# A three-block transformer kernel: the mask of the sparse attention by threshold, rank and scan, and the weight splits before it on another engine

## The chip, the cores and the metric

The kernel runs on one core of one Trainium2 chip. The metric is the device time of one execution in microseconds (us); it was measured three times. An "engine" below is one of the core's five: PE (TensorE, matmuls), DVE (VectorE), ACT (ScalarE), POOL (GpSimd) and SP (SyncE, here only the queue that issues the weight loads).

## The reference

The program computes, for 512 tokens of width 1024, a stack of blocks in float32: an even mixer, a feed-forward layer, an odd mixer, another feed-forward layer, and then two layers of a second block. Only the odd mixer is touched. Cut to what matters:

```python
cq, ckv, kr, ik, iw = _split(h @ w_in, (512, 256, 64, 64, 8))
cq, ckv = _rms_norm(cq, q_norm), _rms_norm(ckv, kv_norm)
qf = (cq @ w_qb).reshape(B, T, 8, 128 + 64)          # per head: nope part, rope part
qi = (cq @ w_iq).reshape(B, T, 8, 64)                # index queries, rope on the first 32
ki = _layer_norm(ik, ik_g, ik_b)                     # index keys, rope on the first 32
def block(c):                                        # 128 queries at a time
    isc = einsum('bqh,bqhs->bqs', wi, relu(einsum('bqhd,bsd->bqhs', qi, ki)))
    isc = where(kpos <= tq, isc, -1e30)
    _, idx = lax.top_k(isc, 128)                     # of equal scores the earliest keys win
    g = kv_cat[idx]
    pr = masked_softmax(einsum('bqhc,bqkc->bqhk', qa, g), idx <= tq)
    return einsum('bqhk,bqkc->bqhc', pr, g[..., :256])
```

Every query may look at its 128 best keys by the index score. The kernel does not gather keys: it computes attention over all earlier keys and adds a mask (0 for a chosen key, -1e30 for another).

## The kernel before

**Weights.** Every product is done as three matmuls on a high and a low part of each operand (lines 595 to 597, `mm3`). SP loads a weight tile into `wraw`, ACT copies its high part to `whi` (line 1318, `split`), and another engine subtracts it to give the low part `wlo`: POOL at line 3128 or DVE at line 2074. Which of the two it is stands in the plan of the weights (`weight_plan`, lines 309 to 399): an item has `low="pool"`, `"dve"` or `"both"`. PE waits for the low part before it uses the tile. Two tiles of 2048 columns fit, so tile n+2 is split once PE has used tile n. Each engine's program walks the same list of items (`Slots`), and `prepare` issues the splits whose buffers are free at that point of that engine's own instruction order; nothing else orders them.

**The odd mixer.** Five programs (`odd` in the tensor, scalar, vector, gpsimd and sync programs) are written out by hand and meet at semaphores. In order:

- `o_in`: the first projection; DVE and POOL then make the index keys (`kk`, slot 1) and the rope part of the keys (slot 0).
- `o_tm`, the index-query half ("iq"): four products of 128 tokens each. ACT copies each out of its bank ("iq raw"), DVE applies the rotation (`rope`, lines 2339 to 2352: six TENSOR_TENSOR and a COPY), PE transposes the result (`turn_index_query`, line 1074) and ACT copies it to `qi`. The raw buffers and the rotated buffers are two deep, so token tile 2 needs the transpose of tile 0.
- `o_tm`, the "q" half: four products more. Transposes of the index queries stand between them. POOL rotates these queries (`rotate`, lines 3157 to 3169, six TENSOR_TENSOR each).
- the transposes of `kk` (line 1067), ACT's copy of the index keys (`kiT`), and index scores for query block 1 (128 queries against 256 keys): per head a small matmul (line 1136), a Relu on ACT into `rl`, a multiply-add on DVE (lines 2873, 2876) into the score rows. Blocks 2 (384 keys) and 3 (512 keys) follow; query block 0 needs no choice.
- `work`: the products with `o_q_nope` (`o_qn`), `o_w_uk` and `o_w_uv`, woven between the index scores.
- `best_keys(q, c)`: 16 rounds of MAX (line 2887, the eight largest of each row) and MATCH_REPLACE (line 2889, overwrites those eight by -3e38 in a copy). After 16 rounds 128 keys are overwritten, and one TENSOR_SCALAR (line 2893) makes the mask from them. Block 1 is done beside the index scores of 2 and 3, block 2 directly after, block 3 one round per head inside the attention loop.
- the attention loop over 32 heads (8 per query block): PE scores (1160, 1161) and mask (1162), DVE row maximum (2922), ACT exponential (1950), PE transpose (1170), a copy by ACT or DVE, PE value product (1182).

## Time and profile before

| what | value |
|---|---|
| median of three runs | 3355.51 us (3355.22 to 3355.51) |
| the profiled execution: its own time, its span in the trace | 3355.51 us, 3353.9 us |
| PE busy, matmuls | 3236.1 us, 96% |
| DVE busy | 2029.2 us, 61% |
| ACT busy | 1457.0 us, 43% |
| POOL busy | 906.4 us, 27% |
| share of the chain that ended last | PE 78%, DVE 16%, ACT 3%, issue 1% |
| the odd mixer's stretch from the iq products to its output projection | about 829 to 1004 us |

Busy time is the time in which an instruction of the engine is recorded, waiting for a port inside an instruction included. The chain goes back from the last instruction to whatever released it. It is a mean over stages: in the feed-forward layers PE is never idle for long, while the odd mixer has waits in both directions, and only that stretch of 175 us is touched here.

### The profile page before, as it was taken

How to read it: one execution, taken by the hardware profiler on the slowest of the kernel's cores; microseconds unless marked ns; L12 is line 12 of the kernel's file. 1: busy time of each engine (PE TensorE's matmuls, PEld its weight loads, DVE VectorE, ACT ScalarE, POOL GpSimd, SP SyncE). 2: the span in 40 equal slices, each digit the busy share in tenths (PEclk: the TensorE clock that was granted, in tenths of full speed). 3: DMA queues.
4: the chain of work that ended last, by engine and by line, in shares of the span. 5: the costliest groups of instructions: out<-in, count | busy, mean ns of one | idle time of the engine just before them, and what ended most of it. 6: DMA issues, size and time to landing. Idle time of an engine off the chain costs nothing.

```text
span 3353.9 us, 47772 instructions
## 1 busy us (share of the span) xinstructions
PE 3236.1 (96%) x20092; PEld 2874.7 (86%) x20092; DVE 2029.2 (61%) x2997; ACT 1457.0 (43%) x2244; POOL 906.4 (27%) x413
## 2 busy tenths in 40 slices
PE   8999999999989999999999999999999999999998
PEld 6887899978668899888999778899899998788998
DVE  6568755445856544575747636574775576366656
ACT  4465445433534444354434324453454343235433
POOL 3210133321400333203232431323232323313232
PEclk9999999999999999999999999999999999999999
DMA  4310333331102333313222322332332323223332
GB/s 131 112 43 26 107 97 117 103 100 58 63 26 88 101 113 101 124 56 123 89 88 95 113 84 77 117 101 82 114 101 86 105 85 122 76 89 107 94 96 76
DMA packets 239815, 308.97 MB, mean 92 GB/s; under 512 B 8337, under 2 KB 168097, under 8 KB 239089
## 3 DMA queue, kind: packets, MB, share of 16 engines
q1 hardware_dynamic: 236016, 291.41, 27.1%
q0 software_dynamic: 3584, 14.52, 1.2%
q8 instruction: 158, 2.59, 0.3%
q14 instruction: 57, 0.46, 0.0%
HBM read 303.80 MB, written 2.10 MB: 91 GB/s over the span
## 4 chain that ended last, share of the span: by engine, by line
PE 78%; DVE 16%; ACT 3%; issue 1%; DMA 0%; POOL 0%; DVEq 0%; ACTq 0%
PE bank L595 24%; PE bank L597 24%; PE bank L596 24%; DVE wlo L2074 3%; ACT whi L1318 1%; DVE wraw L2096 1%; DVE raw_w L2096 1%; PE bank L974 1%; DVE xl L2147 1%; PE bank L615 1%; PE bank L1257 1%; PE bank L1248 1%; DVE ul_w L2274 1%; PE bank L1182 0%; DVE st L2105 0%
## 5 line engine op out<-in xcount | busy, mean ns | idle before, releaser
L3128 POOL TENSOR_TENSOR wlo<-wraw,whi 128x1024 fp32r<-128x1024 f32 (+3 forms) x217 | 555.0, 2561 | 1508.0 <-ACT whi L1318 1507.6
L595 PE MATMUL bank<-xh,whi 128*128 128x256 f32 (+1 forms) x2456 | 724.6, 295 | 48.6 <-DVE zt L2269 20.0
L1318 ACT ACTIVATE whi<-wraw 128x1024 fp32r<-128x1024 f32 (+3 forms) x426 | 440.6, 1038 | 675.8 <-PE bank L597 545.2
L597 PE MATMUL bank<-xh,wlo 128*128 128x256 f32 (+1 forms) x2456 | 718.7, 293 | 0.0
L596 PE MATMUL bank<-xl,whi 128*128 128x256 f32 (+1 forms) x2456 | 715.3, 291 | 0.0
L595 PEld LDWEIGHTS bank<-xh,whi 128*128 128x128 f32 x2456 | 467.3, 190 | 69.9 <-issue 28.8
L3128 POOL TENSOR_TENSOR wlo<-raw_w,whi 128x1024 fp32r<-128x1024 f32 (+1 forms) x130 | 311.6, 2401 | 723.5 <-ACT whi L1318 723.5
L596 PEld LDWEIGHTS bank<-xl,whi 128*128 128x128 f32 x2456 | 468.0, 191 | 10.3
L597 PEld LDWEIGHTS bank<-xh,wlo 128*128 128x128 f32 x2456 | 466.5, 190 | 10.5
L595 PE MATMUL bank<-whi,uh_w 128*128 128x512 f32 x1216 | 473.9, 390 | 0.0
L597 PE MATMUL bank<-whi,ul_w 128*128 128x512 f32 x1216 | 473.4, 389 | 0.0
L596 PE MATMUL bank<-wlo,uh_w 128*128 128x512 f32 x1216 | 473.1, 389 | 0.0
L1318 ACT ACTIVATE whi<-raw_w 128x1024 fp32r<-128x1024 f32 (+1 forms) x315 | 307.8, 979 | 361.6 <-PE bank L597 265.1
L2074 DVE TENSOR_TENSOR wlo<-wraw,whi 128x1024 fp32r<-128x1024 f32 (+2 forms) x209 | 243.8, 1169 | 296.0 <-ACT whi L1318 295.2
L595 PE MATMUL bank<-ah_w,whi 128*128 128x256 f32 x1296 | 367.4, 284 | 10.7 <-DVE wraw L2096 6.8
L595 PE MATMUL bank<-whi,xh 128*128 128x512 f32 (+2 forms) x976 | 371.6, 381 | 4.0 <-DVE xl L2320 2.2
L596 PE MATMUL bank<-al_w,whi 128*128 128x256 f32 x1296 | 366.6, 283 | 0.0
L597 PE MATMUL bank<-ah_w,wlo 128*128 128x256 f32 x1296 | 366.5, 283 | 0.0
L596 PE MATMUL bank<-wlo,xh 128*128 128x512 f32 (+2 forms) x976 | 366.5, 375 | 0.0
L597 PE MATMUL bank<-whi,xl 128*128 128x512 f32 (+2 forms) x976 | 366.4, 375 | 0.0
L2074 DVE TENSOR_TENSOR wlo<-raw_w,whi 128x1024 fp32r<-128x1024 f32 (+1 forms) x185 | 211.8, 1147 | 253.8 <-ACT whi L1318 253.0
L597 PEld LDWEIGHTS bank<-whi,ul_w 128*128 128x128 f32 x1216 | 228.2, 188 | 47.9
(392 smaller groups left out, 5049.0 us busy)
## 6 DMA issues: line engine op xcount, KB each, us to landing
wraw<-in_w_in SPq DMA_DIRECT2D x26, 1024.0 KB, 5.2
wraw<-in_ffn_w_down SPq DMA_DIRECT2D x20, 1024.0 KB, 5.1
raw_w<-in_ffn_w_down SPq DMA_DIRECT2D x20, 1024.0 KB, 5.1
raw_w<-in_mlp_w SPq DMA_DIRECT2D x19, 1024.0 KB, 5.1
wraw<-in_mlp_w SPq DMA_DIRECT2D x17, 1024.0 KB, 5.2
wraw<-in_ffn_w_gate SPq DMA_DIRECT2D x32, 512.0 KB, 4.8
raw_w<-in_ffn_w_gate SPq DMA_DIRECT2D x32, 512.0 KB, 5.0
raw_w<-in_ffn_w_up SPq DMA_DIRECT2D x32, 512.0 KB, 4.5
```

Source lines behind the costliest of these rows:

```text
L595: M.matmul(o, lh, rh, start=start, stop=False, skip_group_check=more)
L596: M.matmul(o, lh, rl, start=False, stop=False, skip_group_check=more)
L597: return M.matmul(o, ll, rh, start=False, stop=stop, skip_group_check=more)
L615: i = M.transpose(bank[:, j * 128:(j + 1) * 128], src[:, (f + j) * 128:(f + j + 1) * 128], ident)
L974: ins = M.matmul(o[:, 0:256], lhs, rhs, start=(br == 0), stop=(br == 2 and kk + 128 >= nk))
L1248: M.matmul(bank[:, 0:n], s.qk[:, 4 + hh, t * 128:(t + 1) * 128], s.qk[:, hh, t * 128:T], start=True, stop=True).then_inc(*made.inc(("made" ...
L1257: i = M.matmul(bank[:, q * 128:(q + 1) * 128], s.PT[:, hh % 2, o:o + 128], s.vt[:, t, hh * 128:(hh + 1) * 128], start=(t == 0), stop=(t == q))
L1318: A.activation(hi, raw, ACT.Copy).then_inc(*k.w_hi.inc(("hi", j)))
L2074: V.tensor_tensor(lo, raw, hi.bitcast(F), ALU.subtract).then_inc(*k.w_lov.inc(("lo", j)))
L2096: V.tensor_tensor(b, x, y, ALU.subtract).then_inc(*done.inc(("sum of", j)))
L2147: V.tensor_tensor(lo, ring.of((*key, f))[:, :].rearrange("p (f t) -> p f t", f=4), hi.bitcast(F), ALU.subtract).then_inc(*done.inc((*name, ...
L3128: G.tensor_tensor(lo[:, 0:n], raw[:, 0:n], hi[:, 0:n].bitcast(F), ALU.subtract).then_inc(*k.w_lo.inc(("lo", j)))
```

## The change

Four things change, all in the odd mixer.

1. The mask. The sixteenth MATCH_REPLACE and the one TENSOR_SCALAR go. In their place nine DVE instructions per query block take the 128th largest score as a threshold, mark the keys above it and count them, mark those equal to it, number the equal ones by a running sum, keep as many as are still wanted, add the two marks, turn them into 0 and -1e30, apply the causal mask to the last 128 keys and convert to bfloat16. They write the two rows of `rl`.
2. The low parts of the second `o_tm` tile and of the first `o_qn` tile, done by DVE before, are done by POOL.
3. PE transposes index-query tile n after product n+2 instead of after product n+3; ACT's copies follow.
4. ACT takes the square roots for `ckv` after the second "q" product instead of after the fourth, and POOL asks for its next weight tile before it rotates query tile 1, not after. On DVE the statistics of `ckv` stand behind the (empty) walk through the "q" products.

```diff
@@ -271,3 +271,3 @@
 
-    def slot(self, tag, view, fine=0, share=False, low="pool"):
+    def slot(self, tag, view, fine=0, share=False):
 
@@ -283,3 +283,3 @@
         else:
-            self.loads[load].items = [self.item(tag, load, 2, 0, nk, "both" if share else low)]
+            self.loads[load].items = [self.item(tag, load, 2, 0, nk, "both" if share else "pool")]
 
@@ -378,5 +378,4 @@
     add_tm("o_tm", kview("o_q_tm"), 512, 1024, fine=0)
-    plan.slot("o_tm", kview("o_q_tm")[:, :, 0:512], low="dve")
-    plan.slot("o_qn", kview("o_q_nope")[:, :, 0:512], low="dve")
-    plan.slot("o_qn", kview("o_q_nope")[:, :, 512:1024])
+    add_tm("o_tm", kview("o_q_tm"), 0, 512, fine=0)
+    add_fm("o_qn", kview("o_q_nope"), 0, 1024, 512)
     add_fm("o_uk", kview("o_w_uk"), 0, 1024, 1024)
@@ -1122,7 +1121,7 @@
         for tt, _ in enumerate(tm_units("o_tm", ("iq",), 512, x, 4)):
-            if tt > 2:
-                turn_index_query(tt - 3)
+            if tt > 1:
+                turn_index_query(tt - 2)
         for tt, _ in enumerate(tm_units("o_tm", ("q",), 512, x, 4)):
-            if tt < 3:
-                turn_index_query(tt + 1)
+            if tt < 2:
+                turn_index_query(tt + 2)
         turn_keys("ki", 1)
@@ -1863,5 +1862,4 @@
         def index_query(key, tt):
-            if tt > 2:
-                turn_index_query(tt - 3)
             if tt > 1:
+                turn_index_query(tt - 2)
                 act.wait_ge(at("iq", tt - 2))
@@ -1910,5 +1908,5 @@
         for tt, _ in enumerate(tm_units("o_tm", ("q",), query)):
-            if tt < 3:
-                turn_index_query(tt + 1)
-            if tt == 3:
+            if tt < 2:
+                turn_index_query(tt + 2)
+            if tt == 1:
                 act.wait_ge(at("o var", 1, 3))
@@ -2857,2 +2855,3 @@
         run(tm_units("o_tm", ("iq",), index_query))
+        run(tm_units("o_tm", ("q",), lambda key, tt: None))
         for tt in range(NT):
@@ -2861,3 +2860,2 @@
             root(tt, 1)
-        run(tm_units("o_tm", ("q",), lambda key, tt: None))
         for tt in range(NT):
@@ -2883,3 +2881,3 @@
             n = (q + 1) * 128
-            full, left, top = isc[q], wkk[:, c, 0:n], o.m8[:, c, :]
+            full, left, top, cn = isc[q], wkk[:, c, 0:n], o.m8[:, c, :], o.cn
             for r in range(16):
@@ -2888,7 +2886,24 @@
                 dve.wait_ge(done.now())
-                V.match_replace(left, top, left if r else full, -3.0e38).then_inc(*done.inc(("left over", q, r)))
                 if r < 15:
+                    V.match_replace(left, top, left if r else full, -3.0e38).then_inc(*done.inc(("left over", q, r)))
                     yield
-            dve.wait_ge(at("left over", q, 15))
-            V.tensor_scalar(o.mb[q], left, -2.0e38, -1e30, ALU.is_gt, ALU.mult).then_inc(*done.inc(("mb", q)))
+            thr = top[:, 7:8]
+            gt, eq = rl[:, 0, 0:n], rl[:, 1, 0:n]
+            V.tensor_scalar(gt, full, thr, 0.0, ALU.is_gt, ALU.add, accum_out=cn[:, 0:1]).then_inc(*done.inc())
+            dve.wait_ge(done.now())
+            V.tensor_scalar(cn[:, 1:2], cn[:, 0:1], -1.0, 128.0, ALU.mult, ALU.add).then_inc(*done.inc())
+            V.tensor_scalar(eq, full, thr, None, ALU.is_equal).then_inc(*done.inc())
+            dve.wait_ge(done.now())
+            V.tensor_tensor_scan(left, o.one[:, :].to_broadcast([128, n]), eq, 0.0, ALU.mult, ALU.add).then_inc(*done.inc())
+            dve.wait_ge(done.now())
+            V.scalar_tensor_tensor(left, left, cn[:, 1:2], eq, ALU.is_le, ALU.mult).then_inc(*done.inc())
+            dve.wait_ge(done.now())
+            V.tensor_tensor(gt, gt, left, ALU.add).then_inc(*done.inc())
+            dve.wait_ge(done.now())
+            V.tensor_scalar(gt, gt, -1.0, 1e30, ALU.add, ALU.mult).then_inc(*done.inc())
+            d = gt[:, n - 128:n]
+            dve.wait_ge(done.now())
+            V.tensor_tensor(d, d, con[:, C_CM:C_CM + 128], ALU.min).then_inc(*done.inc())
+            dve.wait_ge(done.now())
+            V.tensor_copy(o.mb[q], gt).then_inc(*done.inc(("mb", q)))
             yield
@@ -3257,4 +3272,4 @@
         slots.done()
-        rotate(1)
         slots.get("o_qn")
+        rotate(1)
         rotate(2)
```

The order of instructions shows what the plan makes of this. "waits" names the semaphores: `s_w_hi` is ACT's high part, `s_w_lo` the low part from POOL, `s_w_lo_half` the one from DVE. On POOL, behind the rotation of the keys (COPY wkk_o), before:

```order
L3242 COPY wkk_o<-wkk_o 128x4x64 [waits s_pool_out]
L3160 TENSOR_TENSOR gb<-zv_o,cs 128x256 [waits s_act_out]
L3161 TENSOR_TENSOR gb<-zv_o,cs 128x256
L3163 TENSOR_TENSOR X_o<-gb 128x8x32 [waits s_pool_out]
L3165 TENSOR_TENSOR gb<-zv_o,cs 128x256 [waits s_pool_out]
L3166 TENSOR_TENSOR gb<-zv_o,cs 128x256
L3168 TENSOR_TENSOR X_o<-gb 128x8x32 [waits s_pool_out]
L3160 TENSOR_TENSOR gb<-zv_o,cs 128x256 [waits s_dve_out,s_act_out,s_pool_out]
```

And after:

```order
L3257 COPY wkk_o<-wkk_o 128x4x64 [waits s_pool_out]
L3143 TENSOR_TENSOR wlo<-wraw,whi 128x2048 [waits s_w_hi] x2
L3175 TENSOR_TENSOR gb<-zv_o,cs 128x256 [waits s_act_out]
L3176 TENSOR_TENSOR gb<-zv_o,cs 128x256
L3178 TENSOR_TENSOR X_o<-gb 128x8x32 [waits s_pool_out]
L3180 TENSOR_TENSOR gb<-zv_o,cs 128x256 [waits s_pool_out]
L3181 TENSOR_TENSOR gb<-zv_o,cs 128x256
L3183 TENSOR_TENSOR X_o<-gb 128x8x32 [waits s_pool_out]
L3143 TENSOR_TENSOR wlo<-wraw,whi 128x2048 [waits s_w_hi,s_pool_out]
L3175 TENSOR_TENSOR gb<-zv_o,cs 128x256 [waits s_dve_out,s_act_out]
```

Two splits of 2048 columns now stand in front of the rotation of query tile 0 (the first TENSOR_TENSOR on `zv_o`), and the split of the second `o_qn` tile, which stood behind the rotation of tile 1, stands in front of it.

On DVE, from the last copy of the index keys through the rotation of index-query tile 0 (`X_o`), before:

```order
L2822 COPY wkk_o<-wkk_o 128x4x64 [waits s_dve_out]
L2074 TENSOR_TENSOR wlo<-wraw,whi 128x2048 [waits s_w_hi]
L2343 TENSOR_TENSOR rsc_o<-X_o,cs 128x128 [waits s_act_out]
L2344 TENSOR_TENSOR rsc_o<-X_o,cs 128x128
L2346 TENSOR_TENSOR X_o<-rsc_o 128x8x16 [waits s_dve_out]
L2348 TENSOR_TENSOR rsc_o<-X_o,cs 128x128 [waits s_dve_out]
L2349 TENSOR_TENSOR rsc_o<-X_o,cs 128x128
L2351 TENSOR_TENSOR X_o<-rsc_o 128x8x16 [waits s_dve_out]
L2832 COPY X_o<-X_o 128x8x32 [waits s_dve_out]
L2343 TENSOR_TENSOR rsc_o<-X_o,cs 128x128 [waits s_act_out]
```

And after:

```order
L2820 COPY wkk_o<-wkk_o 128x4x64 [waits s_dve_out]
L2341 TENSOR_TENSOR rsc_o<-X_o,cs 128x128 [waits s_act_out]
L2342 TENSOR_TENSOR rsc_o<-X_o,cs 128x128
L2344 TENSOR_TENSOR X_o<-rsc_o 128x8x16 [waits s_dve_out]
L2346 TENSOR_TENSOR rsc_o<-X_o,cs 128x128 [waits s_dve_out]
L2347 TENSOR_TENSOR rsc_o<-X_o,cs 128x128
L2349 TENSOR_TENSOR X_o<-rsc_o 128x8x16 [waits s_dve_out]
L2830 COPY X_o<-X_o 128x8x32 [waits s_dve_out]
L2341 TENSOR_TENSOR rsc_o<-X_o,cs 128x128 [waits s_act_out]
```

The split in front of the rotation is gone (so is a second one in front of tile 3).

On DVE at the end of the choice for query block 1, where `rl_o` holds the marks, `gb` the scores, the threshold and the counts, and `wkk_o` the running sum; before:

```order
L2887 MAX gb<-wkk_o 128x8 [waits s_dve_out]
L2889 MATCH_REPLACE wkk_o<-gb,wkk_o 128x256 [waits s_dve_out]
L2893 TENSOR_SCALAR mb_o<-wkk_o 128x256 [waits s_dve_out]
L2887 MAX gb<-gb 128x8
L2889 MATCH_REPLACE wkk_o<-gb 128x384 [waits s_dve_out]
```

And after (the running sum is printed as a SCALAR_TENSOR_TENSOR on one_o):

```order
L2885 MAX gb<-wkk_o 128x8 [waits s_dve_out]
L2892 TENSOR_SCALAR rl_o,gb<-gb 128x256 [waits s_dve_out]
L2894 TENSOR_SCALAR gb<-gb 128x1 [waits s_dve_out]
L2895 TENSOR_SCALAR rl_o<-gb 128x256
L2897 SCALAR_TENSOR_TENSOR wkk_o<-one_o,rl_o 128x256 [waits s_dve_out]
L2899 SCALAR_TENSOR_TENSOR wkk_o<-wkk_o,gb,rl_o 128x256 [waits s_dve_out]
L2901 TENSOR_TENSOR rl_o<-rl_o,wkk_o 128x256 [waits s_dve_out]
L2903 TENSOR_SCALAR rl_o<-rl_o 128x256 [waits s_dve_out]
L2906 TENSOR_TENSOR rl_o<-rl_o,con 128x128 [waits s_dve_out]
L2908 CAST mb_o<-rl_o 128x256 [waits s_dve_out]
L2885 MAX gb<-gb 128x8
L2888 MATCH_REPLACE wkk_o<-gb 128x384 [waits s_dve_out]
```

Two instructions give way to nine, and all but the third wait for the one before them. Behind them stands the first MAX of block 2 as before; the same happens with 384 and 512 columns.

## Rows read from the trace of the kernel before

**Rows 1.** Waits of PE, 820 to 1010 us: total, times, longest (us).
```profile
PE bank L1182 <- DVE X_o L2325: 6.1, 5, 2.4
PE bank L1136 <- ACT kiT_o L1507: 2.3, 1, 2.3
...
PE bank L1136 <- DVE xl L2320: 1.9, 1, 1.9
```

**Rows 2.** Timeline of PE, 829 to 860 us: start, duration, line, instruction [idle before].
```profile
829.15 0.50 PE L595 MATMUL bank<-whi,xh 128*128 128x512 f32 x1 [2.23 <-DVE xl L2320]
...
840.46 0.60 PE L1074 MATMUL bank<-con,X_o 128*128 128x128 f32 x4
...
853.72 1.04 PE L1067 MATMUL bank<-con,wkk_o 128*128 128x128 f32 x8
857.09 2.00 PE L1136 MATMUL bank<-kiT_o,qo_o 64*128 64x256 f32 x16 [2.34 <-ACT kiT_o L1507]
```

**Rows 3.** Timeline of DVE, 832 to 870 us.
```profile
832.20 0.42 DVE L2814 TENSOR_TENSOR zv_o<-zv_o,par 128x256 f32<-128x256 f32 x1
...
834.90 2.28 DVE L2074 TENSOR_TENSOR wlo<-wraw,whi 128x2048 fp32r<-128x2048 f32 x1
...
838.80 0.30 DVE L2832 COPY X_o<-X_o 128x256 f32<-128x256 f32 x1
...
845.28 0.82 DVE L2343 TENSOR_TENSOR rsc_o<-X_o,cs 128x128 f32<-128x128 f32 x1
...
850.08 0.29 DVE L2832 COPY X_o<-X_o 128x256 f32<-128x256 f32 x1
...
856.78 3.94 DVE L2787 TENSOR_SCALAR zv_o<-zv_o,rs 128x256 f32<-128x256 f32 x1
...
862.02 0.34 DVE L2873 TENSOR_SCALAR gb<-rl_o,wi_o 128x256 f32<-128x256 f32 x1
862.47 4.02 DVE L2876 SCALAR_TENSOR_TENSOR gb<-rl_o,wi_o,gb 128x256 f32<-128x256 f32 x7
```

**Rows 4.** Timeline of POOL, 840 to 905 us.
```profile
844.57 1.39 POOL L3160 TENSOR_TENSOR gb<-zv_o,cs 128x256 f32<-128x256 f32 x1 [12.67 <-ACT zv_o L1507]
...
856.02 4.55 POOL L3128 TENSOR_TENSOR wlo<-wraw,whi 128x2048 fp32r<-128x2048 f32 x1 [0.91 <-ACT whi L1318]
...
887.90 4.64 POOL L3128 TENSOR_TENSOR wlo<-wraw,whi 128x2048 fp32r<-128x2048 f32 x1 [13.61 <-ACT whi L1318]
892.49 1.19 POOL L3160 TENSOR_TENSOR gb<-zv_o,cs 128x256 f32<-128x256 f32 x1
...
900.20 2.41 POOL L3128 TENSOR_TENSOR wlo<-wraw,whi 128x1024 fp32r<-128x1024 f32 x1 [1.44 <-ACT whi L1318]
```

**Rows 5.** Timeline of DVE, 888 to 895 us.
```profile
889.25 4.97 DVE L2876 SCALAR_TENSOR_TENSOR gb<-rl_o,wi_o,gb 128x512 f32<-128x512 f32 x2 [1.56 <-ACT rl_o L1507]
```

**Rows 6.** The last MATCH_REPLACE line: ns min/median/max, first and last start, forms.
```profile
L2889 DVE MATCH_REPLACE8 wkk_o<-gb,wkk_o x45: 407/543/678, 868.4 to 953.0; 128x256 f32<-128x256 f32 x15, 128x384 f32<-128x384 f32 x15, 128x512 f32<-128x512 f32 x15
```

**Rows 7.** Timeline of ACT, 829 to 860 us: the high parts of the two tiles.
```profile
830.67 1.90 ACT L1318 ACTIVATE whi<-wraw 128x2048 fp32r<-128x2048 f32 x1
...
840.71 1.92 ACT L1318 ACTIVATE whi<-wraw 128x2048 fp32r<-128x2048 f32 x1 [0.98 <-PE bank L597]
```

**Rows 8.** The line that made the mask.
```profile
L2893 DVE TENSOR_SCALAR mb_o<-wkk_o x3: 293/360/426, 900.0 to 953.7; 128x256 bf16<-128x256 f32 x1, 128x384 bf16<-128x384 f32 x1, 128x512 bf16<-128x512 f32 x1
```

**Rows 9.** The running sum of the even mixer, the one scan of this form.
```profile
L2427 DVE TENSOR_TENSOR_SCAN og_e<-gb,og_e x1: 1212/1212/1212, 68.7 to 68.7; 4x512 f32<-4x512 f32 x1
```

**Rows 10.** Timeline of DVE, 920 to 960 us, the attention loop.
```profile
923.35 0.29 DVE L2922 TENSOR_REDUCE nm_o<-bank 128x1 f32<-128x128 f32 x1 [2.81 <-PE bank L1162]
...
937.41 0.42 DVE L2922 TENSOR_REDUCE nm_o<-bank 128x1 f32<-128x256 f32 x1 [0.78 <-PE bank L1162]
...
956.36 0.56 DVE L2922 TENSOR_REDUCE nm_o<-bank 128x1 f32<-128x384 f32 x1 [1.56 <-PE bank L1162]
```

**Rows 11.** Stretch: length, busy PE, PEld, DVE, ACT, POOL; granted clock, DMA share, GB/s.
```profile
860.00:880.00 20.00, 17.97 (x63) 11.24 (x64) 18.68 (x51) 8.07 (x18) 4.94 (x7) 0.83 0.09 26
```

More of the change, by code:

```diff
@@ L3257, in odd @@
         slots.done()
+        slots.get("o_qn")
         rotate(1)
-        slots.get("o_qn")
         rotate(2)
```

## Prediction

> **What bounds the kernel now.** The profile's page says PE 96% busy and PE 78% of the last chain, so outside the odd mixer DVE or POOL time costs nothing. I therefore went on with the waits of PE in the mixer's stretch, 820 to 1010 us: it waits for DVE's copy in the attention loop (6.1 us in five waits), for the index keys (2.3 us) and for a DVE result before the index scores of block 2 (1.9 us) [rows 1]. So here the chain jumps between PE and DVE. Next the timelines. From 829.15 the four iq products take 11.31 us, 2.83 each, with no gap; the transposes of the keys start at 853.72 [rows 2]. Up to there PE is dense: whatever holds PE before 853.72 is paid in full. The DVE rows show which operation is late: TENSOR_TENSORs of the rotation of tile 3 take 0.82 us each, and a TENSOR_SCALAR of 256 columns 3.94 us where the same form beside it takes 0.34 [rows 3].
>
> **The mechanism that carries the forecast.** Set these beside POOL. The 3.94 us end at 860.72; POOL's split of 2048 columns runs from 856.02 to 860.57 [rows 3, 4]. At 889.25 two SCALAR_TENSOR_TENSORs take 4.97 us together, and POOL's next split runs from 887.90 to 892.54 [rows 4, 5]. So a DVE instruction of such a form, issued while POOL is inside one instruction, stands until that one ends, whatever its length; when both have a queue they alternate (rotation of tile 3: 845.28 to 850.37, 5.1 us; POOL's own step grows to 1.19 us) [rows 3, 4]. Not all forms are held: MATCH_REPLACE has 678 ns as its longest of 45, though POOL splits at 900.20 beside it [rows 4, 6]. The Trainium skill ("GPSIMD Engine Reference", section "Key points") says that GpSimd shares its SBUF interfaces with VectorE and contends with DVE instructions in a two-port mode or with two SBUF inputs; by that rule TENSOR_SCALAR, copies and the scan are held too, the trace agrees for the first, and no row here shows the scan. It speaks against this change; the terms below would be the same from the rows alone.
>
> **Part 1: two splits from DVE to POOL, and the earlier transposes.** I walk it in the times of before.
> - POOL's first added split starts when ACT's high part ends, 830.67 + 1.90 = 832.57 [rows 7], and takes 4.6 us like its sisters [rows 4]: to about 837.3. DVE is then at the second TENSOR_TENSOR on the index keys (the first ends at 832.62) [rows 3]. The rest of the index keys, up to 834.9, is 2.3 us. It is held and ends at about 839.5. It gains the 2.28 us of the DVE split, which is gone.
> - The rotation of tile 0 takes 2.0 us (tile 1 began as tile 0 ended, at 839.1, after the split's end at 837.2) [rows 3]: ready at 841.5 instead of 839.1. Before, PE asked for it at 840.46 [rows 2]. Now it asks after the third product, at 829.15 + 0.1 + 3 x 2.8 = 837.65. **New wait: 3.9 us.** Behind it in PE's queue stands the fourth iq product, and behind that ACT's next high part, which needs that product.
> - PE: transpose (0.44 with its refill, from 13.26 us for four products and four transposes between 840.46 and 853.72, less the old wait of 0.3), product 3 to 844.8, q product 0 to 848.0, q product 1 to 851.3. Tiles 1 and 2 are rotated at 843.4 and 845.3, in time.
> - ACT's high part for `o_qn` ran 840.71 to 842.63 [rows 7]; it follows product 3, so 845.0 to 846.9. POOL's second added split: 847.0 to 851.6. Raw tile 3 is copied at 847.9, so its rotation meets that split and is held until 851.6. Then POOL starts the rotation of query tile 0 and both alternate, as before, 4.9 us: ready at 856.5. PE has wanted it since 851.3. **New wait: 5.3 us, less the old 0.3.** Together the transposes of the keys move by 3.9 + 5.0 = **8.9 us**.
> - The removed 2 x 2.28 us of DVE are inside this count; DVE waits there anyway. The loads of `o_w_uk` and later tiles now wait for POOL's low part and leave SP about 6 us later; their tile is split at 887.90, over 30 us after the load, so that is hidden. If that cover were gone it would cost those 6 us.
> - The square roots moved earlier let DVE's four scalings finish before the third split (the 3.94 us hold goes). What is late next is the first index score: PE's wait of 2.34 us for the index keys stays (2.1), and the multiply of the first head now meets the third split and is held to its end, moved by 7.3 us. The rotation of tile 1, now behind that split, then runs beside the seven multiply-adds, which took 0.57 each alone [rows 3]; at about 1.1 each for six of them (POOL's 1.19 per step) that adds 3.3 us. 7.3 + 3.3 - 8.9 = **+1.7 us** at PE's wait before block 2. Bounds: -1.6 (no contention) to +4.
>
> **Part 2: the mask.** Prices from rows, for 256 / 384 / 512 columns: TENSOR_SCALAR and the conversion 0.29 / 0.36 / 0.43 [rows 8]; TENSOR_TENSOR 0.42 at 256 and 2.28 at 2048 [rows 3], so 0.55 and 0.69 between; SCALAR_TENSOR_TENSOR 0.50 / 0.62 / 0.75 (0.57 with its gap); a tiny one 0.15; the causal piece 0.29. The scan is 1.21 for 512 [rows 9]; for 256 it lies between 0.61 (all by length) and 1.21, I take 0.68, near the lower end because the fixed part of the TENSOR_TENSOR rows is 0.15, and 0.95 for 384. The count that the first instruction also gives has no row: between 0 and 0.4, I take 0.15. With 0.04 between dependent ones the nine take 3.7 / 4.5 / 5.3 us. Removed are MATCH_REPLACE with its load of 0.09 and the old mask: 0.73 / 1.05 / 1.26 [rows 6, 8]. Net **3.0 / 3.5 / 4.05 us**.
> - Block 1: all but its first two or three instructions meet POOL's split of 900.20, 2.41 us long [rows 4]: another 2.4 (0 to 2.4). Block 2 then ends 3.0 + 2.4 + 3.5 = 8.9 us later. It has 2.81 us of cover: DVE waited that long for PE at 923.35 [rows 10]. So the attention loop starts **6.1 us** late. There DVE is the pace (one MAX and one MATCH_REPLACE per head) and PE follows; DVE waited only 0.78 at 937.41 [rows 10], which I take off: **5.3**.
> - Block 3 stands between the heads 15 and 16: 4.05 us. PE works two heads ahead, and before DVE waited 1.56 at 956.36 [rows 10] just behind it. I take **1.5 us** as what shows, between 0 and 4.05.
> - The marks lie in `rl`; block 1's end comes after the last index score has left it, so no wait is added.
>
> **Part 3: the clock.** In 860 to 880 us the granted clock is 0.83 on average [rows 11], a stretch at 1.2 instead of 2.4 GHz just after PE's 1.9 us wait. Two new waits of 4 and 5 us, and 6 us before the attention loop, invite more of that; 20 x 0.17 / 0.5 = 6.8 us at the lower level cost 3.4 us of dense work there. How often the new waits do so no row says: 0 to 7 us, I take 1.5, since the old stretch may also go.
>
> **Sum.** 8.9 + 1.7 + 5.3 + 1.5 + 1.5 = 18.9 us on the profiled execution's 3355.51, which is also the median of the runs: **3374 us**. Its own range is 3367 to 3381.
>
> **The rivals.**
> - Only the mask costs. If the added splits slip between DVE's instructions, or the transposes are not asked for so early in effect, the first two terms vanish and 5.3 + 1.5 + 1 remain: 3363 us. For it: the meeting at 832.6 is close, both become ready within 0.1 us. Against it: whichever goes first, DVE's next TENSOR_TENSOR is held for the rest.
> - Worse: each new wait brings a stretch of 6.8 us at the lower clock, three times 3.4 us, on top of 17.4: 3383 us. For it: the low stretch [rows 11] follows a wait of only 1.9 us. Against: the waits before 829.15 (2.2 us) and 857.09 (2.3 us) [rows 2] were followed by none.
> - The other side: DVE gains. It loses two splits and the 3.94 us hold, so the index scores of block 1 could start 4 us earlier against PE, the 1.9 us wait and its 3.4 us of low clock vanish, -5.3 us, and the mask costs 2 us behind the 2.81 us cover: 3352 us, not slower. It decides if POOL's splits hold DVE for under 1 us each. The holds of 3.94 us and 4.97 us speak against that [rows 3, 5].
> - The change does nothing measurable: gains of DVE and cost of the mask cancel, 3355 us.
>
> **How the numbers follow.** Forecast 0.58, only the mask 0.18, worse clock 0.12, cancelling 0.08, the DVE gain 0.04. 0.2% of this kernel, 6.7 us, is what a measurement can tell from no change. The last two cases lie within it, save a small tail to the fast side (0.02), and so does a part of "only the mask" at its low end; slower by over 0.2% gets 0.87, the same 0.11. The range takes in the forecast's own, nearly all of "only the mask" and most of the worse clock: 3361 to 3384 us.
>
> **What would show it.** In the changed profile: a PE wait of about 4 us in front of the first index-query transpose and about 5 us in front of the fourth, both for DVE's `X_o`; DVE instructions of the index keys or of tile 3's rotation with 3 to 4.6 us durations that end with a POOL split; the transposes of the keys near 862.6; a scan near 0.7, 0.95 and 1.2 us; nine instructions of 3.7, 4.5 and 5.3 us, the first set longer by the hold; no DVE wait before head 0 but a PE wait of about 6 us. Wrong if the keys' transposes stand before 858, if POOL's splits end before DVE's rotation starts, or if the attention loop starts less than 10 us later than before.

## The result, and the profile after

The changed kernel takes 3377.7 us (median of four, 3374.95 to 3380.44), the kernel before 3355.51: ratio 1.0063, 95% interval 1.0051 to 1.0076, about 21 us slower (17 to 26). The profiled execution of it took 3375.52 us; its span is 3374.2 us, 20.3 above the span before. The prediction was 3374 us, range 3361 to 3384, slower by over 0.2%.

To compare traces I count from one mark, the first transpose of keys and values (825.01 us before, 826.61 after): the code up to there is the same, and what differs there is the clock: a stretch at half of it begins at 725 us in both traces and lasts 6.9 us after the change, 3.4 before. From the mark to each place, in us:

| place | before | after | difference | forecast |
|---|---|---|---|---|
| the transposes of the keys | 28.7 | 38.85 | +10.1 | +8.9 |
| first index score of block 2 | 38.4 | 49.5 | +11.1 | +10.6 |
| first row maximum of the attention loop | 98.3 | 112.7 | +14.4 | +16.7 |
| end of the loop (first product of the output) | 178.6 | 198.9 | +20.3 | +18.9 |

The 20.3 us lie between the mark and the end of the loop, where the forecast had put them; the 1.6 us by which the mark is late come back behind the loop. The portions are others: from block 2's first score to the first row maximum the forecast had 6.1 us and the trace shows 3.3, inside the loop it had 2.2 and the trace shows 5.9. Those two errors nearly cancel.

PE's timeline after (start, duration, line, instruction, idle before and its releaser):

```profile
843.00 0.66 PE L1073 MATMUL bank<-con,X_o 128*128 128x128 f32 x4 [2.05 <-DVE X_o L2830]
...
857.28 1.11 PE L1073 MATMUL bank<-con,X_o 128*128 128x128 f32 x4 [4.37 <-DVE X_o L2830]
...
865.46 1.03 PE L1066 MATMUL bank<-con,wkk_o 128*128 128x128 f32 x8
868.65 1.64 PE L1135 MATMUL bank<-kiT_o,qo_o 64*128 64x256 f32 x6 [2.16 <-ACT kiT_o L1506]
```

Before, the transposes stood at 840.46 and on with no such wait [rows 2]. The two new waits are there, 2.05 and 4.37 us, both for DVE's rotated tile. DVE and POOL at that place:

```profile
834.25 4.89 DVE L2814 TENSOR_TENSOR zv_o<-zv_o,par 128x256 f32<-128x256 f32 x1
...
849.46 3.84 DVE L2341 TENSOR_TENSOR rsc_o<-X_o,cs 128x128 f32<-128x128 f32 x1 [2.65 <-ACT X_o L1506]
...
861.02 0.35 DVE L2785 TENSOR_SCALAR zv_o<-zv_o,rs 128x256 f32<-128x256 f32 x1
```

```profile
834.24 4.62 POOL L3143 TENSOR_TENSOR wlo<-wraw,whi 128x2048 fp32r<-128x2048 f32 x1 [0.76 <-ACT whi L1317]
848.54 4.61 POOL L3143 TENSOR_TENSOR wlo<-wraw,whi 128x2048 fp32r<-128x2048 f32 x1 [9.69 <-ACT whi L1317]
```

POOL's added split starts at 834.24 and ends at 838.86; DVE's instruction of 834.25, the second of two equal ones (0.42 us before [rows 3]), ends at 839.14. POOL's second added split, 848.54 to 853.15, holds the first TENSOR_TENSOR of tile 3's rotation: 3.84 us, to 853.30, where the same form takes 0.28 us when free. The scaling at 861.02 is free again, as forecast (3.94 before [rows 3]).

The nine instructions of block 3 in DVE's timeline, and what follows:

```profile
968.33 0.75 DVE L2892 TENSOR_SCALAR_CACHE_REDUCE rl_o<-gb 128x512 f32<-128x512 f32 x1
969.00 0.08 DVE L2892 DVE_READ_ACCUMULATOR rl_o<-gb 128x1 f32 x1
969.12 0.15 DVE L2894 TENSOR_SCALAR gb<-gb 128x1 f32<-128x1 f32 x1
969.19 0.48 DVE L2895 TENSOR_SCALAR rl_o<-gb 128x512 f32<-128x512 f32 x1
969.71 1.23 DVE L2897 TENSOR_TENSOR_SCAN wkk_o<-one_o,rl_o 128x512 f32<-128x512 f32 x1
970.97 0.75 DVE L2899 SCALAR_TENSOR_TENSOR wkk_o<-wkk_o,gb,rl_o 128x512 f32<-128x512 f32 x1
971.75 0.69 DVE L2901 TENSOR_TENSOR rl_o<-rl_o,wkk_o 128x512 f32<-128x512 f32 x1
972.48 0.43 DVE L2903 TENSOR_SCALAR rl_o<-rl_o 128x512 f32<-128x512 f32 x1
972.94 0.29 DVE L2906 TENSOR_TENSOR rl_o<-rl_o,con 128x128 f32<-128x128 f32 x1
973.27 0.43 DVE L2908 CAST mb_o<-rl_o 128x512 bf16<-128x512 f32 x1
...
979.33 0.56 DVE L2937 TENSOR_REDUCE nm_o<-bank 128x1 f32<-128x384 f32 x1 [4.38 <-PE bank L1161]
```

5.3 us as forecast, the scan 1.23. But DVE's next wait for PE is 4.38 us (it was 1.56 [rows 10]), because PE ran dry in between. Two of PE's waits in the loop:

```profile
PE bank L1169 <- ACT X_o L1948: 4.5, 2, 4.2
PE bank L1181 <- ACT X_o L1506: 3.3, 1, 3.3
```

The 4.2 us stand ahead of the first head's transpose, the 3.3 us are behind the nine instructions of block 3. And the granted clock, in stretches of 4 us (as in [rows 11]):

```profile
856.00:860.00 4.00, 2.72 (x9) 2.34 (x10) 3.74 (x12) 0.60 (x1) 1.80 (x3) 0.50 0.38 151
940.00:944.00 4.00, 1.76 (x7) 1.09 (x7) 3.90 (x11) 1.02 (x6) 0.00 (x0) 0.55 0.00 0
944.00:948.00 4.00, 3.57 (x17) 3.44 (x18) 3.67 (x11) 1.25 (x6) 0.00 (x0) 0.50 0.00 0
976.00:980.00 4.00, 4.00 (x12) 2.51 (x12) 0.67 (x2) 0.07 (x1) 0.00 (x0) 0.50 0.00 0
```

Behind its waits of 4.37, 4.17 and 3.26 us PE works at 1.2 in place of 2.4 GHz. From the mark to the end of the loop 30.9 us lie at the lower level after the change, and 10.3 us before. Over the same stretch PE has no matmul for 29.4 us, and had none for 15.5 before. The lower level takes half of the work that PE does in it, 12.6 us after and 5.1 before by an estimate from the two. So of the 20.3 us roughly 14 are idle time and 7 are the clock.

One new wait of PE was in no part of the forecast: 1.72 us at 910 us, for the query tile that POOL rotates behind its split of 899.5. It costs nothing here: the schedule without the new mask has it too, and takes 69.4 us from the keys' transposes to the first row maximum, the kernel before 69.6.

### The profile page after: what moved, and what is told of

Its sections match the earlier page's. It is cut to its first block, busy times and chain, and to the rows that moved or that the text cites. A ratio compares the mean times of both kernels' runs of the same rounds, so it can differ in the third digit from the quotient of the medians.

```text
span 3374.2 us, 47791 instructions
## 1 busy us (share of the span) xinstructions
PE 3242.6 (96%) x20092; PEld 2880.5 (85%) x20092; DVE 2044.1 (61%) x3016; ACT 1457.6 (43%) x2244; POOL 915.4 (27%) x415
## 4 chain that ended last, share of the span: by engine, by line
PE 77%; DVE 18%; ACT 3%; issue 2%; DMA 0%; POOL 0%; DVEq 0%; ACTq 0%
PE bank L594 24%; PE bank L596 23%; PE bank L595 23%; DVE wlo L2072 3%; ACT whi L1317 1%; DVE wraw L2094 1%; PE bank L973 1%; DVE raw_w L2094 1%; DVE wkk_o L2888 1%; DVE gb L2885 1%; PE bank L614 1%; DVE xl L2145 1%; DVE uv_x L3019 1%; PE bank L1256 1%; PE bank L1247 1%
## 5 line engine op out<-in xcount | busy, mean ns | idle before, releaser
L3143 POOL TENSOR_TENSOR wlo<-wraw,whi 128x1024 fp32r<-128x1024 f32 (+3 forms) x219 | 564.2, 2580 | 1537.3 <-ACT whi L1317 1536.9
L595 PEld LDWEIGHTS bank<-xl,whi 128*128 128x128 f32 x2456 | 466.5, 190 | 10.2
L2072 DVE TENSOR_TENSOR wlo<-wraw,whi 128x1024 fp32r<-128x1024 f32 (+1 forms) x207 | 239.0, 1157 | 295.0 <-ACT whi L1317 294.2
L594 PE MATMUL bank<-ah_w,whi 128*128 128x256 f32 x1296 | 367.4, 284 | 11.1 <-DVE wraw L2094 6.8
```

The costliest lines, as they stand in the source:

```text
L594: M.matmul(o, lh, rh, start=start, stop=False, skip_group_check=more)
L595: M.matmul(o, lh, rl, start=False, stop=False, skip_group_check=more)
L2072: V.tensor_tensor(lo, raw, hi.bitcast(F), ALU.subtract).then_inc(*k.w_lov.inc(("lo", j)))
L3143: G.tensor_tensor(lo[:, 0:n], raw[:, 0:n], hi[:, 0:n].bitcast(F), ALU.subtract).then_inc(*k.w_lo.inc(("lo", j)))
```

## The experiments

Each was timed beside the kernel before; a ratio less 1, times 3356 us, gives the difference. Differences to the changed kernel are those of two such ratios, each good to about 4 us, so such a difference is good to about 6 us, and I use it with the traces. A trace is one execution, and where its low stretches of the clock fall differs from one to the next. "Loop" is the time from the first row maximum to the end of the attention loop in its trace: 80.2 us before, 86.1 after.

### The new mask alone

```diff
 # vector program, best_keys, in the kernel before: as in the change
-                V.match_replace(left, top, ...)          # also for r == 15
-            V.tensor_scalar(o.mb[q], left, -2.0e38, -1e30, ALU.is_gt, ALU.mult)
+            # the nine instructions, for blocks 1, 2 and 3
```

> The kernel before with only the new end of the selection (the nine instructions in place of the last MATCH_REPLACE and the old mask) in all three blocks. Theory 'the terms add': what is put behind DVE's 2.81 us of cover before the attention loop is 3.0 + 2.4 + 3.5 = 8.9 us, so 5.3 us of the loop's start and between 1.5 and 4 us at block 3, some low clock on top: 7 to 11 us slower than before, 3362.5 to 3366.5. Rival 'the mask is most of it, the schedule edits little': 14 us or more, 3370 and up. Rival 'hidden': the loop is PE's and swallows it: under 4 us.

Measured: 3368.0 us, ratio 1.0036 (1.0023 to 1.0048), 12 us slower, just above the 7 to 11 expected. The first row maximum is 7.0 us later from the mark, of which 1.5 were there at the transposes of the keys already (a low clock at 832 us, which no edit precedes), the loop takes 84.7 us.

```profile
905.65 2.78 DVE L2899 TENSOR_TENSOR_SCAN wkk_o<-one_o,rl_o 128x256 f32<-128x256 f32 x1
...
929.66 0.61 DVE L2894 TENSOR_SCALAR_CACHE_REDUCE rl_o<-gb 128x384 f32<-128x384 f32 x1
...
934.07 0.28 DVE L2939 TENSOR_REDUCE nm_o<-bank 128x1 f32<-128x128 f32 x1
```

```profile
905.45 2.43 POOL L3145 TENSOR_TENSOR wlo<-wraw,whi 128x1024 fp32r<-128x1024 f32 x1 [1.47 <-ACT whi L1318]
```

The scan of 256 columns, 0.69 us when free, takes 2.78: held by POOL's split up to 907.88. So the block 1 tail is 5.7 us long (4.98 more than the old one), the block 2 tail 4.4 (3.35 more); less the 2.81 us of cover that is 5.5, and 7.0 - 1.5 = 5.5 is what the trace shows. That part of the sum was right (6.1). The rest, 4.5 us, comes inside the loop, where the forecast had 2.2 with the clock.

### The schedule alone

```diff
 # the changed kernel, best_keys as in the kernel before
-            # the nine instructions
+            V.tensor_scalar(o.mb[q], left, -2.0e38, -1e30, ALU.is_gt, ALU.mult)
```

> The changed kernel with the old end of the selection (16th MATCH_REPLACE and one TENSOR_SCALAR): the splits on POOL, the earlier transposes and the other order of roots and rotations alone. Theory 'the terms add': the keys' transposes about 10 us later as in the changed kernel, the start of index scores of block 2 about 10 us later, nothing given back: 10 to 13 us slower, 3365.5 to 3368.5. Rival 'DVE makes up for it': the index scores and selection of block 1 are DVE's, DVE has less to do, and half comes back before the attention loop: 4 to 6 us slower.

Measured: 3367.2 us, ratio 1.0036 (1.0022 to 1.0050), 12 us slower, as expected.

```profile
841.23 0.66 PE L1073 MATMUL bank<-con,X_o 128*128 128x128 f32 x4 [3.41 <-DVE X_o L2830]
...
846.07 0.60 PE L1073 MATMUL bank<-con,X_o 128*128 128x128 f32 x4
...
857.04 1.11 PE L1073 MATMUL bank<-con,X_o 128*128 128x128 f32 x4 [4.36 <-DVE X_o L2830]
```

Here, with the clock full at 830 us, the waits can be set against the forecast: 3.41 us (3.9) and 4.36 (5.3). Between the transposes of 841.23 and 846.07 lie 4.84 us, 1.6 more than the 3.23 of before: the clock fell behind the first wait. The keys' transposes are 11.9 us later: PE is idle for 7.7 us more, and the rest comes from 10.3 us in two stretches at the lower level. Of this 1.2 us come back by the end of the loop. The rival that half comes back is out.

### The splits alone, the earlier transposes alone

```diff
 # splits_pool: weight_plan of the kernel before
-    plan.slot("o_tm", kview("o_q_tm")[:, :, 0:512], low="dve")
-    plan.slot("o_qn", kview("o_q_nope")[:, :, 0:512], low="dve")
+    plan.slot("o_tm", kview("o_q_tm")[:, :, 0:512])
+    plan.slot("o_qn", kview("o_q_nope")[:, :, 0:512])
```

> The kernel before with its two DVE splits given to POOL, and nothing else: transposes of the index queries one product later as before, roots and rotations in the old order. Theory 'hold and earlier request only together': DVE's rotation of tile 0 is held to 841.5, asked for at 840.5, 1 us of PE wait; tile 3's rotation held to 847.2 and then beside POOL's, ready at 852, asked for at 853: nothing. 1 to 3 us slower. Rival 'the holds by POOL alone are the cost': 8 us or more slower, as in the changed kernel. Rival 'DVE gains by two splits less': 1 us or more faster.

```diff
 # turns_only: tensor and scalar program of the kernel before
-            if tt > 2:
-                turn_index_query(tt - 3)
+            if tt > 1:
+                turn_index_query(tt - 2)
...
-            if tt < 3:
-                turn_index_query(tt + 1)
+            if tt < 2:
+                turn_index_query(tt + 2)
```

> The kernel before with only the earlier transposes of the index queries (each right behind the second product after its own, not the third), splits on DVE, roots and rotations in the old order. Theory 'hold and earlier request only together': tile 0 asked for at 837.7 and ready at 839.1 (1.4 us wait), ACT's high part behind the fourth product 1.7 us later and so DVE's split, tile 3 ready at 851.6 and asked for at 848.7 (2.9 us): 3 to 5 us slower. Rival 'the request is the whole cause': 8 us or more. Rival 'PE gets the transposes out of the way': no slower.

Measured: splits 3360.5 us, ratio 1.0013 (1.0004 to 1.0022), 4.4 us slower; transposes 3364.2 us, 1.0018 (1.0009 to 1.0027), 6 us. Both are above what was expected (1 to 3 and 3 to 5). PE's rows, of the splits and then of the transposes, and between them what held DVE in the first:

```profile
849.09 0.66 PE L1074 MATMUL bank<-con,X_o 128*128 128x128 f32 x4 [1.23 <-DVE X_o L2832]
...
853.46 0.65 PE L1074 MATMUL bank<-con,X_o 128*128 128x128 f32 x4 [0.92 <-DVE X_o L2832]
```

```profile
843.72 4.58 DVE L2351 TENSOR_TENSOR X_o<-rsc_o 128x128 f32<-128x128 f32 x1
```

```profile
843.50 4.65 POOL L3128 TENSOR_TENSOR wlo<-wraw,whi 128x2048 fp32r<-128x2048 f32 x1 [6.61 <-ACT whi L1318]
```

```profile
855.35 0.66 PE L1074 MATMUL bank<-con,X_o 128*128 128x128 f32 x4 [2.90 <-DVE X_o L2831]
```

The 2.9 us of the second were in the expectation to the tenth, the 1.4 us at tile 0 are missing. The splits cost more than expected: the wait that I put at tile 0 stands at tile 2 (1.23 us), and the one that I put at nothing, tile 3, is 0.92. Behind the held index keys tile 2's rotation starts 1.8 us later from the mark, so its last TENSOR_TENSOR meets POOL's second split and is held for 4.58 us.

New waits are 2.1 us with the splits alone, 2.9 with the transposes alone and 7.8 with both. The three can't be set side by side as they are: in the profiled executions of the two single edits a low stretch of the clock, at 828 and at 833 us, made PE about 1.4 us late at the first transpose, which hid a wait there. With the clock full at that place the same requests cost 1.33 and 2.90 us, together 4.2 (next experiment). Against 2.1 + 4.2 the 7.8 us leave at most 1.5 for the two edits taking each other's slack. At the first transpose it can be seen: before, tile 0 was ready at 839.10 and PE asked for it at 840.46 [rows 2, 3], a slack of 1.4 us that either edit alone could use, and both together only once. The timed differences (4.4, 6, together 12) are too wide to show it.

### The changed kernel with its splits back on DVE

```diff
 # weight_plan of the changed kernel
-    add_tm("o_tm", kview("o_q_tm"), 0, 512, fine=0)
-    add_fm("o_qn", kview("o_q_nope"), 0, 1024, 512)
+    plan.slot("o_tm", kview("o_q_tm")[:, :, 0:512], low="dve")
+    plan.slot("o_qn", kview("o_q_nope")[:, :, 0:512], low="dve")
+    plan.slot("o_qn", kview("o_q_nope")[:, :, 512:1024])
```

> The changed kernel with its two added POOL splits given back to DVE; earlier transposes, order of roots and rotations and the new mask stay. Theory 'a held rotation costs more where it is asked for earlier': the splits are worth more here than the 4 us that they cost alone: 6 to 8 us faster than the changed kernel, 3370 to 3372. Rival 'independent': 4 us faster, 3374. Rival 'only the earlier request': no faster than the changed kernel.

Measured: 3370.8 us, ratio 1.0037 (1.0023 to 1.0051) against 1.0063: some 9 us faster than the changed kernel. PE's waits for the rotated tiles:

```profile
841.50 0.66 PE L1074 MATMUL bank<-con,X_o 128*128 128x128 f32 x4 [1.33 <-DVE X_o L2831]
854.30 1.11 PE L1074 MATMUL bank<-con,X_o 128*128 128x128 f32 x4 [2.90 <-DVE X_o L2831]
```

They fall from 6.4 to 4.2 us, and the transposes of the keys come 4.4 us earlier from the mark; the same splits alone moved them by 3.7. The other 3.0 us that this trace gains lie inside the attention loop (83.1 against 86.1 us), which the edit does not touch: the wait of 3.26 us behind block 3 is there as before, but the clock stays full behind it. So the timed 9 us don't show that the splits are worth more here than alone.

### POOL's splits in pieces

```diff
 # gpsimd program, split(j), changed kernel
-        G.tensor_tensor(lo[:, 0:n], raw[:, 0:n], hi[:, 0:n].bitcast(F), ALU.subtract)
+        step = 512 if item.tag in ("o_tm", "o_qn", "o_uk", "o_uv") else n
+        for a in range(0, n, step):
+            b = min(a + step, n)
+            G.tensor_tensor(lo[:, a:b], raw[:, a:b], hi[:, a:b].bitcast(F), ALU.subtract)
```

> The changed kernel with POOL's low-part splits of the odd mixer's tiles issued in pieces of 512 columns (about 1.15 us each from 4.6 for 2048) instead of whole. Theory 'a DVE instruction stands until POOL's one instruction ends': no DVE instruction is longer than about 1.5 us, the index keys and rotations of tiles 0 and 3 come 2 to 3 us earlier each, 3 to 6 us faster than the changed kernel: 3372 to 3375. Rival 'the port is POOL's as long as it has work': durations and holds sum to the same, no change, 3377. Rival 'each piece costs POOL a start of its own and delays PE's weight tiles': slower than the changed kernel.

Measured: 3372.5 us, ratio 1.0046 (1.0033 to 1.0059), some 5 us faster than the changed kernel by the ratios, which is within their error. POOL and DVE:

```profile
832.53 5.25 POOL L3146 TENSOR_TENSOR wlo<-wraw,whi 128x512 fp32r<-128x512 f32 x4 [0.34 <-ACT whi L1317]
```

```profile
832.28 0.42 DVE L2812 TENSOR_TENSOR zv_o<-zv_o,par 128x256 f32<-128x256 f32 x1
832.74 1.39 DVE L2814 TENSOR_TENSOR zv_o<-zv_o,par 128x256 f32<-128x256 f32 x1
834.17 1.20 DVE L2341 TENSOR_TENSOR rsc_o<-zv_o,cs 128x64 f32<-128x64 f32 x1
835.29 1.33 DVE L2342 TENSOR_TENSOR rsc_o<-zv_o,cs 128x64 f32<-128x64 f32 x1
836.65 1.21 DVE L2344 TENSOR_TENSOR wkk_o<-rsc_o 128x64 f32<-128x64 f32 x1
837.89 0.22 DVE L2346 TENSOR_TENSOR rsc_o<-zv_o,cs 128x64 f32<-128x64 f32 x1
```

The longest DVE instruction is 1.39 us in place of 4.89, and the four beside the four pieces last 1.2 to 1.4 each: one DVE instruction per piece. So the hold does end with POOL's instruction, whatever its length. But the queue gains only three instructions of 0.22 us, and the four pieces take 5.25 us where the whole split took 4.62: PE's first wait is 3.38 us, as with whole splits (3.41). The fourth transpose waits 3.27 in place of 4.37. From the mark to the end of the loop this trace is only 1.3 us shorter than that of the changed kernel; another 1.7 us lie ahead of the mark, where the code is the same. A gain of 5 us from the pieces is not shown.

### Block 3 alone, and block 3 spread out

```diff
 # mask_b3: kernel before, the nine instructions in the third call only
-        best = best_keys(3, 1)
+        best = best_keys_rank(3, 1)
```

> The kernel before with the nine instructions in block 3 only (between heads 15 and 16); blocks 1 and 2 keep the old end. The forecast's term, PE works two heads ahead and most is covered: 1.5 us slower, 3358. Revised theory from the run with all three (from the first head's row maximum to the end of the loop it took 84.7 us against 80.2): the whole 4.0 us net of DVE time shows, plus a little of low clock: 4 to 5 us slower, 3360.5 to 3361.5.

```diff
 # after_spread: changed kernel, behind the third, fourth, fifth and sixth of the nine
+            if q == 3:
+                yield
```

> The changed kernel with block 3's nine instructions spread over heads 15 to 19 instead of between 15 and 16; they are needed at head 24 and DVE waits for PE by 1.4 to 2.2 us at each head from 16 on. Revised theory, block 3's tail shows in full where it stands: 3.5 to 4.5 us faster than the changed kernel, 3373 to 3374. By the forecast's term of 1.5 us: 3376.

Measured: block 3 alone 3362.3 us, ratio 1.0012 (1.0003 to 1.0021), 4 us slower, its loop 85.9 us; spread out in the changed kernel 3372.7 us, ratio 1.0041 (1.0028 to 1.0054), some 7 us faster than the changed kernel, its loop 79.6 us. PE's waits for ACT's copy and the clock of block 3 alone, then the same waits of the spread version:

```profile
PE bank L1182 <- ACT X_o L1507: 3.6, 2, 3.3
```

```profile
960.00:964.00 4.00, 4.00 (x11) 2.51 (x12) 0.09 (x1) 0.28 (x2) 0.00 (x0) 0.50 0.00 0
```

```profile
PE bank L1181 <- ACT X_o L1506: 0.3, 1, 0.3
```

The wait for ACT's copy is 3.6 us with the tail in one piece (the longest 3.3) and 0.3 spread out, where DVE puts each piece into its own idle time. With the wait goes the low clock behind it: 976 to 980 us are at 0.50 in the changed kernel, at 1.00 in the spread one. The loops of the changed kernel and of the spread one differ by 6.5 us, those of block 3 alone and of the kernel before by 5.7. The 1.5 of the forecast is too low against both. The revised 4 to 5 are below both too, but agree with the timed 4 us (1 to 7) of block 3 alone: its executions lie between 3359 and 3365 us, and the profiled one, at 3363.6, is among the longer.

### The order of roots, splits and rotations alone

```diff
 # scalar program
-            if tt == 3:
+            if tt == 1:
                 act.wait_ge(at("o var", 1, 3))     # and the square roots
 # gpsimd program
-        rotate(1)
         slots.get("o_qn")
+        rotate(1)
 # vector program: the walk through the "q" products ahead of the statistics of ckv
+        run(tm_units("o_tm", ("q",), lambda key, tt: None))
         for tt in range(NT):
...
-        run(tm_units("o_tm", ("q",), lambda key, tt: None))
```

> The kernel before with only the order edits: the square roots at the second q product, POOL's fourth split ahead of its rotation of tile 1, DVE's banks of the q half taken ahead of the statistics loop. Theory from the comparison of the parts (block 2's first index score 0.9 us later against the keys' transposes, 1.1 us back before the attention loop): within 1 us of before. Rival 'DVE gains': the 3.94 us hold is gone and with it PE's wait of 1.9 us and its low clock, 3 to 5 us faster. Rival: the new hold of the first index multiply costs 3 us or more.

Measured: 3357.3 us, ratio 1.0001 (0.9993 to 1.0010): nothing, as expected. The first index score waits 2.98 us for the index keys' copy instead of 2.34; the 3.94 us hold is gone, and the first multiply takes 2.24 us in place of 0.34 [rows 3]. What is freed is taken again 2 us later; DVE gains nothing. The first score of block 2 comes 1.7 us later from the mark, and by the end of the loop 0.4 us are earlier. PE's row and DVE's:

```profile
857.61 2.99 PE L1136 MATMUL bank<-kiT_o,qo_o 64*128 64x256 f32 x16 [2.98 <-ACT kiT_o L1507]
```

```profile
859.15 2.24 DVE L2873 TENSOR_SCALAR gb<-rl_o,wi_o 128x256 f32<-128x256 f32 x1 [3.36 <-ACT rl_o L1507]
```

### Block 3's rounds at other heads of the kernel before

```diff
 # vector program, attention loop
-            next(best, None)
+            if n % 4 != 3:                                       # before_spread
+            if n % 2 if n < 8 else n > 15 or n % 4 != 3:         # before_spread2
+                next(best, None)
```

> The kernel before with block 3's 16 rounds and its mask over heads 0 to 20 (none at every fourth head) instead of one at each of heads 0 to 15. DVE sets the pace up to head 15 and waits 1.4 to 2.2 us per head behind it; four rounds of 1.4 us leave its stretch. PE's waits for DVE's copy in the loop are 6.1 us before. Theory 'DVE's queue is what PE waits for': 3 to 5 us faster, 3351 to 3353.5. Rival 'the waits are latencies of the chain PE, DVE, ACT, PE at the loop's start': under 1.5 us. Rival: head 24 waits for the later mask: slower.

> As the run before it, but with fewer rounds where heads are short: at every second of heads 0 to 7, three of four of heads 8 to 15, each of heads 16 to 21. Six rounds of 1.4 us leave DVE's stretch, and the first eight heads come near PE's own pace (about 1.2 us per head): 1 to 2 us faster than the run before it. Rival: the mask, ready behind head 21, is late for PE, which works two heads ahead: no faster or slower.

The third of these is the first with POOL's splits in pieces of 512 columns, as above.

> The run before_spread with POOL's low-part splits of the odd mixer in pieces of 512 columns. In the changed kernel pieces moved the fourth transpose by 1.1 us, and the first not at all, since DVE passes one instruction per piece. Here the 3.94 us hold of one scaling (two more behind it) and the 4.97 us of two multiply-adds stand beside splits: 0 to 2 us faster than without pieces. Rival: each piece delays POOL's own split (5.2 us from 4.6) and the tile with it: 0 to 1 us slower.

Measured: the first 3358.1 us, ratio 1.0005 (0.9996 to 1.0014), no gain where 3 to 5 us were expected; with pieces 3356.7 us, 0.9999 (0.9990 to 1.0008), no different from either within the error; the second 3350.5 us, ratio 0.9983 (0.9974 to 0.9992), 6 us faster than before, more than expected: the one version that beats both kernels. Waits of PE in the loop, of the first and the second, and the granted clock of the second and of before:

```profile
PE bank L1182 <- DVE X_o L2325: 4.9, 5, 2.4
```

```profile
PE bank L1182 <- DVE X_o L2325: 2.5, 4, 0.9
```

```profile
932.00:940.00 8.00, 6.79 (x44) 5.59 (x43) 6.97 (x20) 3.39 (x14) 0.00 (x0) 1.00 0.00 0
```

```profile
932.00:936.00 4.00, 2.59 (x13) 2.43 (x13) 3.90 (x12) 1.52 (x8) 0.00 (x0) 0.72 0.00 0
```

The first leaves the wait of 2.4 us ahead of the first value product as it is: the round of head 0 stands there. Its waits for DVE fall from 6.1 to 4.9 us, but its loop has 6.8 us at the lower clock where the kernel before has 3.5, and takes as long (80.1 us). The second has no round at head 0, its longest wait is 0.9, and the clock stays at 1.00 in the whole loop, where it was 0.72 at 932 to 936 us in the kernel before. Its loop takes 74.8 us in place of 80.2. The rival that the mask behind head 21 comes late is out.

## Why the prediction was right, and which terms were off

The direction, the place and the two main mechanisms, the hold and the mask's extra time on DVE, were right. That the sum came within 4 us of the measured time is in part luck: the forecast had 17.4 us in waits and DVE time and 1.5 in the clock, the trace shows about 14 and 7.

- **The hold.** Right. DVE's instructions end just behind POOL's split (839.14 and 838.86; 853.30 and 853.15), and the pieces show that its length sets it. The rule that I took from the Trainium skill ("GPSIMD Engine Reference", "Key points") for the scan had no row before; the scan of 2.78 us beside POOL's split agrees with it.
- **The two waits, 3.9 and 5.3 us.** 3.41 and 4.36 at full clock; in the profiled execution of the changed kernel 2.05 and 4.37, because PE came late to the first by a low clock at 831 us. The transposes of the keys were forecast at 862.6 and stand at 865.46, which is 863.9 when the 1.6 us of the mark are taken off. Waits smaller than forecast, a later place: the difference is the clock, at 1.2 GHz from 831.2 to 834.6 us and from 855.1 to 861.9. The transposes are 10.1 us later from the mark, about 6 of them by waits and 4 by the clock.
- **The index scores, +1.7 us.** +0.95 up to block 2's first score.
- **The mask ahead of the loop, 6.1 us.** 5.5 with the mask alone; 4.5 between the schedule alone (110.0 us from the mark, 40.6 to the keys) and the changed kernel (112.7 and 38.85). The scan at 0.69, 0.96 and 1.23 us was forecast at 0.68, 0.95 and 1.21, the nine at 3.7, 4.5 and 5.3; free of POOL they take 3.6, 4.4 and 5.3. The hold in block 1 was 2.4 forecast, 2.1 in the mask alone and 1.0 in the changed kernel, where DVE came 1.2 us behind the split's start:

```profile
911.63 1.33 DVE L2895 TENSOR_SCALAR rl_o<-gb 128x256 f32<-128x256 f32 x1
912.99 0.69 DVE L2897 TENSOR_TENSOR_SCAN wkk_o<-one_o,rl_o 128x256 f32<-128x256 f32 x1
```

```profile
910.41 2.40 POOL L3143 TENSOR_TENSOR wlo<-wraw,whi 128x1024 fp32r<-128x1024 f32 x1
```

  In the changed kernel the old mask would have been held too (its TENSOR_SCALAR takes 1.40 and 1.56 us in the schedule alone, 0.29 and 0.36 when free), so what the new one adds is less; and DVE's cover ahead of the loop was 0.47 us there, not 2.81. The two errors nearly cancel.
- **Block 3, 1.5 us.** Mis-sized. I took DVE's wait of 1.56 us and PE's lead of two heads as cover. PE's lead is used up within the 5.3 us, since it needs each head's row maximum: 3 us of wait, and 3.4 from 6.8 us more at the lower clock, together 6.5 (86.1 against 79.6 us of loop). The upper bound of 4.05 was too low, as it was made of DVE time alone. The clock's part is not always there: with the splits back on DVE the same wait of 3.26 us stands in the same place, and the clock stays full.
- **The clock, 1.5 us.** The term that was furthest off, also apart from block 3. 20.6 us more lie at the lower level, which costs about 7 us of work and at most 10.3. I had taken 1.5 out of bounds of 0 to 7, since the old stretch might also go; the trace lies at their top. The old one did go, but five stretches are there where before there were two. The rival of 3383 us said that each new wait of PE brings a stretch at the lower level, 10.2 us in all; by mechanism it was nearer to what happened than the forecast. It came out 5 us too high: it stood on the forecast's 17.4 us of waits, and took 10.2 for a clock that cost about 7 more than before.
- **The other rivals.** "Only the mask costs" falls: the schedule alone costs 12 us. "DVE gains" falls: the order alone is worth nothing and the splits are a loss.

Open stays why low stretches of the clock appear at 725 and 831 us in some executions and not in others, ahead of any edit. In the fourteen traces, with the same code up to there, the mark lies between 824.0 and 828.7 us.

## What to carry to other kernels

Work that moves from a waiting engine to one whose instructions hold it (DVE beside POOL's splits here, 4.89 us for an instruction of 0.42) is not off the first engine: ask which instruction stands beside it, and how late the consumer asks. Two edits that draw on the slack of one hand-over must be priced together: tile 0 was ready 1.4 us early, and there is one such slack for both. A block of work on an engine that feeds PE once per step goes in pieces into that engine's own waits; in one piece it costs the wait and, in most of these traces, the clock behind it. And before two traces are compared, lay their low stretches side by side: one of 3.4 us ahead of the first transpose hid 1.4 us of the wait there (2.05 in place of 3.41).

## What the runs showed of the hardware

- The traces of the kernel before and of the thirteen others hold 17 waits of PE of 3.19 to 5.26 us in the mixer's stretch. Behind 16 of them the mean granted clock of the next 3 us was below 0.97; behind the 60 waits of 1.5 to 3.0 us it was so in 34, of which 5 stand in a stretch that was low already. It is 0.50, that is 1.2 in place of 2.4 GHz, for 3.4 to 10.3 us at a time, and can fall within the wait: at 855.1 us in the changed kernel, in the wait of 852.9 to 857.3. The same wait does not always do it: the one of 3.26 or 3.27 us behind block 3 was followed by 0.50 in four traces and by 1.00 in one, 2.36 us at head 0 by 1.00 before and by 0.50 with block 3 alone. That the waits cause it was not tried by itself: no run put a wait there and changed nothing else.
- A held DVE instruction ends with POOL's current instruction: 4.89 us beside one of 4.62, four of 1.2 to 1.4 us beside four of 1.3. TENSOR_TENSOR (0.42 us when free), SCALAR_TENSOR_TENSOR (4.97 us for two [rows 5], 0.75 for one when free), TENSOR_SCALAR (3.94 us in place of 0.34 [rows 3]) and the scan (2.78 us in place of 0.69) are all held.
- A TENSOR_SCALAR that also gives its row sum took 0.48, 0.61 and 0.75 us for 256, 384 and 512 columns, plus a read of 0.08; the scan 0.69, 0.96 and 1.23.
